# A block of U transposed by VectorE in 32x32 squares instead of by TensorE, in a decoder layer with product-key experts

## The reference, cut to what matters

```python
def block(tb):
    q = (tb @ w_q).reshape(nt, PEER_HEADS, 2, PEER_DK)
    sc = jnp.einsum('thcd,hcnd->thcn', q, keys)
    s1, i1 = lax.top_k(sc[:, :, 0], PEER_TOPK)
    s2, i2 = lax.top_k(sc[:, :, 1], PEER_TOPK)
    cand_s = s1[..., :, None] + s2[..., None, :]      # 16 x 16 sums a head
    top_s, j = lax.top_k(cand_s.reshape(nt, PEER_HEADS, -1), PEER_TOPK)
    eid = jnp.take_along_axis(cand_i, j, axis=-1)
    g = jax.nn.softmax(top_s, axis=-1)
    act = jax.nn.gelu(jnp.einsum('thkd,td->thk', u[eid], tb), approximate=False)
    return jnp.einsum('thk,thkd->td', g * act, v[eid])
```

## Time and profile before

| | |
|---|---|
| median of 3 runs | 3649.49 us (3648.81 to 3653.74) |
| the profiled execution | 3645.04 us, its span 3643.2 us |
| TensorE busy | 3373.2 us, 93% of the span |
| VectorE, ScalarE, GpSimd busy | 1736.0, 1467.0, 1059.1 us (48%, 40%, 29%) |
| mean granted TensorE clock | 0.943 of full |
| HBM | 206 GB/s over the span |

### The profile page before, as it was taken

How to read it: one execution, slowest core, us unless ns; L and a number is a source line. 1 busy time by engine, 2 the same in 40 slices (tenths; PEclk the granted TensorE clock), 3 DMA queues, 4 the chain that set the end, 5 groups by cost and what they waited for, 6 DMA issues and landing times. The chain is left out here.

```text
span 3643.2 us, 58753 instructions
## 1 busy us (share of the span) xinstructions
PE 3373.2 (93%) x23240; PEld 3097.5 (85%) x23240; DVE 1736.0 (48%) x2388; ACT 1467.0 (40%) x2057; POOL 1059.1 (29%) x763
## 2 busy tenths in 40 slices
PE   7999997968889786799799999999999899999998
PEld 7999996748878776799799999999999877777776
DVE  5344443432210002464437645565554477777764
ACT  5333222114512233442426666565565433333332
POOL 0000000005513343000106775666668711111100
PEclk9999997659988797899899999999999999999999
DMA  6544443325443532566434447888888798889874
GB/s 202 186 161 161 161 162 98 98 95 159 145 169 120 195 106 68 191 200 197 130 123 155 158 163 246 313 287 286 313 277 310 291 367 309 314 313 331 312 239 158
DMA packets 397704, 753.22 MB, mean 207 GB/s; under 512 B 57149, under 2 KB 334941, under 8 KB 347454
## 3 DMA queue, kind: packets, MB, share of 16 engines
q1 hardware_dynamic: 375838, 610.44, 49.9%
q0 software_dynamic: 18432, 134.23, 9.9%
q10 hardware_dynamic: 3264, 6.29, 0.5%
HBM read 690.86 MB, written 59.51 MB: 206 GB/s over the span
## 5 line engine op out<-in xcount | busy, mean ns | idle before, releaser
L2425 POOL TENSOR_TENSOR peer_uT_low<-peer_uT,peer_uT_high 128x512 fp32r<-128x512 f32 x420 | 555.1, 1352 | 393.1 <-ACT peer_uT_high L2463 387.6
L944 POOL TENSOR_TENSOR gate_low<-gate_raw,gate_high 128x512 fp32r<-128x512 f32 x192 | 245.0, 1300 | 1162.6 <-ACT gate_high L900 1162.4
L2306 PE MATMUL banks<-x_high,peer_uT_high 128*128 128x224 f32 x2048 | 473.4, 280 | 0.0
L2307 PE MATMUL banks<-x_low,peer_uT_high 128*128 128x224 f32 x2048 | 463.7, 274 | 0.0
L2307 PEld LDWEIGHTS banks<-x_low,peer_uT_high 128*128 128x128 f32 x2048 | 393.2, 192 | 0.0
L2306 PEld LDWEIGHTS banks<-x_high,peer_uT_high 128*128 128x128 f32 x2048 | 393.1, 192 | 0.0
L227 PE MATMUL banks<-x_high,win_high 128*128 128x288 f32 (+1 forms) x1312 | 349.1, 296 | 0.0
L228 PE MATMUL banks<-x_low,win_high 128*128 128x288 f32 (+1 forms) x1312 | 348.7, 295 | 0.0
L2463 ACT ACTIVATE peer_uT_high<-banks 128x512 fp32r<-128x512 f32 x512 | 306.7, 629 | 0.0
L197 ACT ACTIVATE win_high<-win_raw 128x2048 fp32r<-128x2048 f32 x84 | 160.8, 1915 | 334.2 <-DVEq L190 329.0
L2434 POOL DMA_INDIRECT peer_area<-in_peer_v_dram,peer_expert_row x64 | 136.1, 2127 | 462.3 <-DVE peer_area L2651 449.1
(11 more groups left out here) (385 smaller groups left out, 7385.4 us busy)
## 6 DMA issues: line engine op xcount, KB each, us to landing
peer_u<-in_peer_u_dram SPq DMA_DIRECT2D x128, 1024.0 KB, 5.2
win_raw<-in_w_in_dram SPq DMA_DIRECT2D x38, 2048.0 KB, 8.1
peer_area<-in_peer_v_dram SPq DMA_DIRECT2D x64, 1024.0 KB, 5.9
peer_u<-in_peer_v_dram SPq DMA_DIRECT2D x64, 1024.0 KB, 5.7
gate_raw<-in_w_in_dram SPq DMA_DIRECT2D x96, 512.0 KB, 4.1
w_raw<-in_w_up_ret_dram SPq DMA_DIRECT2D x8, 2048.0 KB, 9.1
w_raw<-in_w_out_dram SPq DMA_DIRECT2D x8, 2048.0 KB, 8.1
w_raw<-in_peer_w_q_dram SPq DMA_DIRECT2D x8, 2048.0 KB, 8.1
```

The costliest lines, as they stand in the source:

```text
L944: pool.tensor_tensor(self.low[:, p % 2, c, :, :], self.raw[:, p % 4, :, c * P:(c + 1) * P], self.high[:, p % 2, c, :, :], ALU.subtract).th ...
L2306: pe.matmul(out, UH[:, c, k, :], XH[:, k, 0:DENSE], start=(k == 0), stop=False)
L2307: pe.matmul(out, UH[:, c, k, :], XL[:, k, 0:DENSE], start=False, stop=False)
L2425: pool.tensor_tensor(UL[:, m % 2, 4 * b:4 * b + 4, :], UT[:, 4 * b:4 * b + 4, :], UH[:, m % 2, 4 * b:4 * b + 4, :], ALU.subtract).then_inc ...
```

## The change

U is loaded in four transfers, each of 32 partitions: partition 32g + e holds, of the rows 32E + e (E = 0 to 3), the columns 512g to 512g + 511. VectorE transposes squares of 32x32 within each group of 32 partitions, half a block at a time, into `UT`, which becomes a double buffer in SBUF; the columns of U then lie in another order over partitions and tiles. The same order is given to the rows of x (`move_rows` copies h within SBUF by 16 transfers, the norm reads the copy), to the query weights (`QuadrantWeightStream`, four transfers a load) and to the norm's gain. ScalarE makes only `UH`, in two halves of 128x1024; GpSimd makes all of `UL`, in two halves. TensorE transposes nothing of U. `SECOND` is made by ScalarE, as relu(1 - |iota - index|), in two steps. The picks are spread over about 65 blocks, with transposes between their operations (`worked`), and the weights' layout starts at block 67. 12 dots lie among the picks, 44 behind them, the last 8 dots and all 64 row sums in the V stage. The picks' temporaries move into the large area, and the second buffer of `GH` and `GL` into that of x.

```diff
-                    for c in range(2):
-                        sp.dma_start(U[:, c, :], u_in[c]).then_inc(u_loaded[c], 16)
...
                 def load_u(m):
-                    sp.wait_ge(turned, after(4 * (m - 2) + 4))
-                    sp.dma_start(U[:, m % 2, :], u_in[m]).then_inc(u_loaded[m % 2], 16)
+                    sp.wait_ge(turned, after(2 * (m - 2) + 2))
+                    for g in range(4):
+                        sp.dma_start(U_PARTS[32 * g:32 * g + 32, m % 2, :, :], u_in[g, m]).then_inc(u_loaded[m % 4], 16)
...
+                def turn(h):
+                    m, b = divmod(h, 2)
+                    if b == 0:
+                        dve.wait_ge(u_loaded[m % 4], after(64 * (m // 4) + 64))
+                    dve.wait_ge(low, after(2 * (m - 2) + b + 1))
+                    cols = slice(b * HALF * 32, (b + 1) * HALF * 32)
+                    dve.transpose(UT[:, m % 2, b * HALF:(b + 1) * HALF, :].rearrange("p c (E e) -> p E c e", E=4),
+                                  U_PARTS[:, m % 2, :, cols].rearrange("p E (c i) -> p E c i", i=32)).then_inc(turned, 1)
+
+                def half_block():
+                    h = next(halves)
+                    turn(h)
+                    for g in dots_at(h):
+                        dot(g)
+
+                def worked(t, weight):
+                    work[0] += weight
+                    while work[1] < PICK_HALVES[t] * work[0] // PICK_TOTAL:
+                        work[1] += 1
+                        half_block()
...
+                for m in range(sum(PICK_HALVES) // 2 + 1 - TURNS_AHEAD, BLOCKS):
+                    if m + TURNS_AHEAD < BLOCKS:
+                        half_block()
+                    for q in spread_at(m + 1):
+                        if q == 0:
+                            dve.wait_ge(sel_ready, after(2))
+                        hot_rows(q)
+                    if m + TURNS_AHEAD < BLOCKS:
+                        half_block()
...
                 def high(m):
-                    for b in range(4):
+                    for b in range(2):
...
-                        act.activation(UH[:, m % 2, 4 * b:4 * b + 4, :], tiles, ACT.Copy).then_inc(uT_high, 1)
+                        act.activation(UH[:, m % 2, part, :], UT[:, m % 2, part, :], ACT.Copy).then_inc(uT_high, 1)
...
+                def low_halves(m):
+                    for b in range(2):
+                        pool.wait_ge(uT_high, after(2 * m + b + 1))
                         if b == 0:
                             pool.wait_ge(hidden_done, after(m - 1))
...
+                        pool.tensor_tensor(UL[:, m % 2, part, :], UT[:, m % 2, part, :], UH[:, m % 2, part, :], ALU.subtract).then_inc(low, 1)
...
+                def second(q):
+                    b = q % 2
+                    act.wait_ge(placed, after(q - 1))
+                    for j in range(4):
+                        t = 4 * q + j
+                        ins = act.activation(SECOND[:, b, j, :], iota[:], ACT.Abs, bias=SEL[:, 1, t:t + 1], scale=-1.0)
+                    ins.then_inc(distances, 1)
+                    act.wait_ge(distances, after(q + 1))
+                    act.activation(SECOND[:, b, :, :], SECOND[:, b, :, :], ACT.Relu, bias=1.0, scale=-1.0).then_inc(second_ready, 1)
...
+def move_rows(sp, area, hT, g, moved):
+
+    by_row = area[:, A_QT:A_QT + KT * T].rearrange("p (r q t) -> p q r t", q=4, t=T)
+    for q in range(4):
+        sp.dma_start(by_row[32 * g:32 * g + 32, q, :, :], hT[32 * q:32 * q + 32, 4 * g:4 * g + 4, :]).then_inc(moved, 16)
...
+DOTS = ((52, 130, SLOTS * 3 // 16), (130, 248, SLOTS - SLOTS // 8 if SPARSE > NEW else SLOTS))
+DOTS_END, SUMS_FROM, SUMS_END = 12, 16, 108
```

More of the change, by code:

```diff
@@ L1 @@
+import itertools
 import math
@@ L234, in product, with by_quadrant, load @@
         last.then_inc(self.product_done, 1)
+def by_quadrant(rows):
+    return rows.rearrange("(g c i) n -> g i c n", g=4, i=32)
+class QuadrantWeightStream(WeightStream):
+    def load(self, sp, i, b, columns, first=False):
+        if not first:
+            sp.wait_ge(self.low_ready, after(self.UNITS * i - self.UNITS + 2 * b + 2))
+        for g in range(4):
+            sp.dma_start(self.raw[32 * g:32 * g + 32, b, :, :], columns[g]).then_inc(self.loaded[b], 16)
 def decoder_step_kernel(nc, A, O):
@@ L2108, with dots_done @@
[L2108 to L2118 removed]
+def dots_done(h):
+    done = 0
+    for first, last, count in DOTS:
+        if h >= first:
+            done += up_to(count - done, first, last, h)
+    return done
@@ L2121, in peer, with spread_at @@
+def spread_at(m):
+    return range(spread_before(m), spread_before(m + 1))
 def peer(nc, G, area, XH, XL, spilled, keys_loaded):
```

456 lines of the change are left out of this document (208 added, 248 removed).

## The result

| | before | after |
|---|---|---|
| median of six runs | 3652.11 us (3648.81 to 3654.62) | 3673.18 us (3665.01 to 3689.58) |
| ratio, 95% interval | | 1.0062 (1.004 to 1.0084) |
| profiled execution | 3645.04 us | 3689.58 us |
| TensorE, VectorE, GpSimd busy | 93, 48, 29% | 88, 56, 31% |
| mean granted TensorE clock | 0.943 | 0.913 |

The change made the kernel slower by 21 us. The forecast was 3564, faster with a chance of 0.86: wrong in sign, and outside its range.

A forecast was written before the change was run, and what follows sets the result against it. TensorE was taken to bound the kernel before, and GpSimd's port with VectorE to decide after the change; 3643.2 - 85 (U stage) - 8 (start) + 8 (V stage) = 3558 span, 3564 us as median, range 3440 to 3630.

The forecast's parts named there:

- TensorE's gain, 227 us of turnings to be had: U stage: TensorE bounds it, and dropping 128 turnings of 1.77 us frees 227 us if nothing else takes its place.
- The turn at 1.22 us, outside the port: U stage, VectorE: each half-block transpose takes 1.22 us, 2.45 a block, without holding the port shared with GpSimd.
- Rival D: U stage: slower, because the turn holds the port too or costs twice; 3846 us if it holds it; chance 0.10.
- The port: U stage: GpSimd's subtractions and VectorE's two-input operations exclude one another; 6.15 us a block first half, 7.3 to 8.2 second.
- The load: U stage: four 32-partition transfers cost 4.8 us of DMA a block instead of 2.5; period at least 5.8, then 6.5 to 7.2.
- three resources come out close together: U stage: 5.8 to 6.15 us a block first, 7.2 to 8.2 second; taken as 6.3 and 7.7, 896 us, -85.
- Start: Opening of the U stage: first product at 1920.5 instead of 1928.5 us, -8.
- Moves: Before the last stage: 16 transfers moving h's rows within SBUF cost 0, with 2 us of cover.
- V stage: After the U stage: more gathers and 8 dots inside, 360 GB/s just fits; charged +8, bounds 0 and +40.
- The clock: U stage: if TensorE's clock leaves its upper level in gaps, products exceed 5.33 us a block and the forecast is too fast.
- The signs I had named: U stage: turns 1.2 us, GpSimd over 90% busy, dots 3 to 4 us, DMA share above 0.9, TensorE 85% and 80%.
- C: U and V stages: everything serial, 6.7 and 8.2 us a block, V +28; 3642 us, reaching down to 3600; chance 0.12.

The follow-up runs named there:

- k1: Against h1, each dot of a gathered row with x became a plain one-input sum over 2048 columns; 3519.00 us (0.9633).
- m2: Changed kernel, with x's rows copied into idle PSUM banks and the dots from block 32 on reading them there; 3650.09 us (0.9985).
- h2: As h1, but the dots of gathered rows with x taken over 64 of 2048 columns; 3497.51 us (0.9579).
- h1: Changed kernel, with one 128-partition transfer per block of U and gelu blocks stored from ScalarE's own queue; 3596.63 us (0.9844).
- e1: Changed kernel, with each gelu block's store issued by ScalarE itself instead of by SyncE behind the loads of U; 3666.85 us (1.0028).
- k5, k3: One of the follow-up kernels with the change; the text does not say which edit or time belongs to this label.
- m1: Changed kernel with gelu stores from ScalarE's queue, second low half of blocks 64 to 127 on VectorE, and dots reading x from PSUM; 3617.62 us (0.9895).
- e2: Changed kernel, with each block of U loaded by one transfer of 128 partitions, 8 KB a partition; 3598.10 us (0.9858).

## Why the prediction was wrong, point by point

- **TensorE's gain, 227 us of turnings to be had**: right; it was given away again, and 36 us more.
- **The turn at 1.22 us, outside the port**: 1.23, and beside GpSimd's pair it keeps its 1.24. Rival D falls.
- **ScalarE no bound**: right.
- **The port**: the mechanism was right (k1: 78 us; m2), its size too small. I added the dots as 2.28 us each to GpSimd's sum. But an instruction that meets a busy port stands through what the other has running, at 2649 us even a pair of 2.4 us each, and then what is queued behind it stands too: the dots took 2.90 us in the mean, and the small compares 0.97, not the 0.26 that I charged (less than their median of 0.335 in the earlier trace rows); TensorE waited 85 us for them. GpSimd's half, where the dots stay out of its way, takes the 2.45 that I gave it (2.46 in m2); beside them it takes 2.71.
- **The load**: the rate was near. In the kernel before with narrow loads the DMA engines were busy for 0.82 x 487 / 61 = 6.5 us a block (4147 of 4348 matmuls are 61 of 64 blocks) against 0.63 x 487 / 64 = 4.8: 1.7 more, where I had 2.3. The reading was wrong. I set its period (5.8 us first, 6.5 to 7.2 or 7.3 second) beside the port's (6.15; 7.3 to 8.2) and took roughly the larger, "three resources come out close together". They are links of one loop: a turn waits for the load, the dot and the one-hots stand in front of the next turn, the next load waits for that turn. Measured, the load costs 62 to 93 us and the dots 76 to 99, nearly whichever way the other stands. **This is the step that failed**: 6.3 and 7.7 us a block were taken as a little above the maximum of terms that lie in one loop; they came out at 6.8 and 9.0. The U stages of the profiled executions show the terms laid one on another: 822 us (h2, wide load, short dots), 922 with the full dots (h1), 991 with the narrow load as well (e1), 1011 in the changed kernel. That each of the two has its price beside the other is measured; the loop as the reason is read from the waits and from the lists.
- **The order of SyncE's queue**: the gelu store behind the loads was missing from my list; it made the longest wait of the profile and cost about 6 us (e1, the intervals overlap), at full width none (h1).
- **Start**: -6.8 against -8. **Moves**: +5.4 against 0. In the changed kernel the last add is at 1783.2, the eight copies are issued until 1786.2, and the norm's engines meet only behind them (the page's SyncE queue):

```profile
1776.56 9.64 SPq L1919 DMA_DIRECT2D peer_area<-h_T  x8
1786.84 3.83 SPq L1988 DMA_DIRECT2D ffn_gain<-in_norm_ffn_w_dram  x4
```

  I had priced their transfer, with 2 us of cover, not the stage's opening that stands behind their issue. This stretch comes in two lengths: 252.7 to 252.9 us in nine of the seventeen other kernels with the change (e1, h1, k5 and m1 among them), 250.0 to 250.3 in seven (e2, k1 and m2 among them), 251.8 in k3. Why is open.
- **V stage**: -3.5 against +8; 364 GB/s at a share of 0.96 from 3200 to 3400, "just fits" held.
- **The clock** left its upper level in the gaps, as named: the products came out longer than the 5.33 us a block that my sum had. From first to last gelu the same 6613 or so matmuls hold TensorE for 833 us in the changed kernel (granted 0.90), 803 with the wide load (e2, 0.94) and 770 with short dots too (h2, 0.97); the 967 us of before, less 227 of turning, would be about 740. So of the 188 us between the U stages of h2 and the changed kernel up to 63 can be slower products, a consequence of the gaps that lengthens them in turn. The prices of the load and of the dots contain their share of it; no run took the clock apart from them.
- **The signs I had named**: turns at 1.23 us and TensorE busy for 87 and 79% came. GpSimd over 90% busy, dots at 3 to 4 us and a DMA share above 0.9 in the second half did not: GpSimd was busy for 79 and 69% of the two windows, the dots took 2.90, the share was 0.85. By my own rule ("If GpSimd is idle more than a fifth while TensorE waits, the lock is not the cause") the port would have been ruled out, and k1 shows that it costs 78 us. In a loop no link needs to be busy all the time, so that sign could not tell.
- **Rivals**: C had the right picture (everything serial, 3642). Its first half was right (6.7 us a block, measured 6.8), its second 0.8 us a block too low (8.2 against 9.0), its V stage 31 us too high (+28 against -3.5); together it was 31 us too low, with a chance of 0.12. It too charged a dot of 2.28 us with 2.28 us. The chance of slower, 0.11, hung on the turn alone; no rival let the load and the port together cost more than the turnings gave.

## What to carry to other kernels

When work leaves the bounding engine, write the loop that it joins (load, turn, copies, free buffer) and add what stands in it; a table of busy sums per engine gives the floor, not the period. Price a load by the partitions that it reaches: 32 in place of 128 took the DMA engines from 0.63 to 0.82 of the time at TensorE's old rhythm, and cost 62 to 93 us here, 78 in the kernel before, which TensorE bounds. And count VectorE's instructions with two SBUF inputs beside GpSimd, and short ones such as the compares, by what they stand through and not by their own length; a second operand in an idle PSUM bank took the dots off the port without changing the result. Gaps in TensorE's work also slow the work that is left (833 us for what took 770). The longest wait of a profile can be slack: e1 took 462 us of it away for 6.

## What the runs showed that was not expected

- Runs of 2 KB cost nothing at 128 partitions (3598.44 against 3598.10), but 13 us at 32 (3673.18 against 3659.71, intervals 1.0040 to 1.0084 and 1.0013 to 1.0033).
- A transfer to 128 partitions whose source has an outermost dimension of 4 left the DMA engines at a share of 0.32 and made the changed kernel 618 us slower, a cure worse than the narrow load.
- A gather on GpSimd (0.95 us in the median) takes 2.83 us beside a two-input instruction of VectorE: all eight long ones of the U stage begin during a dot or another operation with two SBUF inputs.
